# Four taps of chunk 6's depthwise convolution on TensorE, and the diagonals of chunk 7 made in another split

## The reference, cut to what matters

```python
def causal_depthwise_conv(x, buf, w, b):          # width 31, one filter per channel
    xp = jnp.concatenate([buf.astype(x.dtype), x], axis=1)
    y = lax.conv_general_dilated(xp, w[:, None, :], window_strides=(1,), padding='VALID',
                                 dimension_numbers=('NWC', 'WIO', 'NWC'), feature_group_count=ch)
    return y + b, xp[:, -(width - 1):, :]

def conformer_conv(h, buf, w_in, w_dw, b_dw, ln_g, ln_b, w_out):
    a, gate = jnp.split(h @ w_in, 2, axis=-1)
    u = a * jax.nn.sigmoid(gate)
    u, tail = causal_depthwise_conv(u, buf, w_dw, b_dw)
    u = layernorm(u, ln_g, ln_b)
    return jax.nn.silu(u) @ w_out, tail
```

## Time and profile before

| | us |
|---|---|
| median of 3 runs | 1502.82 |
| lowest, highest | 1500.53, 1505.07 |
| the profiled execution | 1500.38 |
| its span | 1498.8 |
| TensorE busy | 1458.5 (97%) |
| VectorE busy | 979.2 (65%) |
| ScalarE busy | 908.6 (61%) |

### The profile page before, as it was taken

The page is one execution under the profiler, slowest core; times in us unless marked ns, Lnnn a source line. Parts: engine busy times, 40 slices in busy tenths (PEclk is TensorE's granted clock), DMA queues, the critical chain, the costliest instruction groups (busy, mean ns, idle before and its releaser), DMA issues.

```text
span 1498.8 us, 28447 instructions
## 1 busy us (share of the span) xinstructions
PE 1458.5 (97%) x11276; PEld 1348.6 (90%) x11276; DVE 979.2 (65%) x1475; ACT 908.6 (61%) x1658; POOL 269.9 (18%) x469
## 2 busy tenths in 40 slices
PE   5999999999999999999999989999999999999998
PEld 4788669999999999999889856679999999999997
DVE  4799966878744878645546356664887744767643
ACT  4699877877633776535435556664767643666633
POOL 2489810000000332100000022210000000322200
PEclk9999999999999999999999999999999999999999
DMA  9887683355554454653437366653255554455653
GB/s 379 307 303 270 249 283 127 95 165 170 183 175 143 159 165 162 194 172 127 127 107 259 114 225 225 226 198 118 80 175 168 177 177 153 145 168 167 198 165 100
DMA packets 72118, 273.50 MB, mean 182 GB/s; under 512 B 8065, under 2 KB 10129, under 8 KB 71601
## 3 DMA queue, kind: packets, MB, share of 16 engines
q1 hardware_dynamic: 65824, 247.69, 49.0%
q0 software_dynamic: 5872, 23.64, 4.6%
q10 hardware_dynamic: 288, 0.35, 0.1%
HBM read 262.80 MB, written 8.85 MB: 181 GB/s over the span
## 4 chain that ended last, share of the span: by engine, by line
PE 85%; DVE 8%; ACT 3%; issue 2%; DMA 2%; SPq 0%; DVEq 0%; ACTq 0%
PE ps L739 68%; DVE ps L1896 4%; PE ps L1004 3%; PE ps L713 2%; PE ps L1076 1%; PE ps L1082 1%; PE ps L1059 1%; DMA ada_w<-w_ada_dram 1%; PE ps L1143 1%; PE ps L1095 1%; PE ps L1110 1%; PE ps L809 1%; PE ps L919 1%; ACT w_att L1631 1%; ACT w_hi L1287 1%
## 5 line engine op out<-in xcount | busy, mean ns | idle before, releaser
L1727 DVE TENSOR_TENSOR w_lo<-raw,w_hi 128x1024 fp32r<-128x1024 f32 (+1 forms) x296 | 387.4, 1310 | 229.5 <-ACT w_hi L1287 229.3
L739 PE MATMUL ps<-h_hi,w_hi 128*128 128x288 f32 x1920 | 524.9, 298 | 1.7 <-DVE h_lo L1801 1.7
L739 PE MATMUL ps<-h_lo,w_hi 128*128 128x288 f32 x1920 | 518.9, 294 | 0.0
L1287 ACT ACTIVATE w_hi<-raw 128x1024 fp32r<-128x1024 f32 (+1 forms) x309 | 347.0, 1124 | 108.1 <-PE ps L739 73.5
L739 PEld LDWEIGHTS ps<-h_hi,w_hi 128*128 128x128 f32 x1920 | 360.3, 188 | 7.9 <-DVE h_lo L1801 4.5
L739 PEld LDWEIGHTS ps<-h_lo,w_hi 128*128 128x128 f32 x1920 | 360.0, 187 | 1.1 <-issue 0.2
L739 PE MATMUL ps<-h_hi,w_lo 128*128 128x288 f32 x1920 | 312.4, 294 | 0.0
L739 PEld LDWEIGHTS ps<-h_hi,w_lo 128*128 128x128 f32 x1920 | 274.5, 188 | 0.0
L739 PE MATMUL ps<-act_hi,w_hi 128*128 128x288 f32 x704 | 193.2, 296 | 0.0
L739 PE MATMUL ps<-act_lo,w_hi 128*128 128x288 f32 x704 | 193.0, 297 | 0.0
L739 PEld LDWEIGHTS ps<-act_hi,w_hi 128*128 128x128 f32 x704 | 132.5, 188 | 0.0
(11 more groups left out here) (265 smaller groups left out, 2071.1 us busy)
## 6 DMA issues: line engine op xcount, KB each, us to landing
raw<-w_k_dram SPq DMA_DIRECT2D x245, 512.0 KB, 3.5
raw<-w_down_dram SPq DMA_DIRECT2D x64, 704.0 KB, 4.1
ada_w<-w_ada_dram SPq DMA_DIRECT2D x71, 512.0 KB, 5.8
k_page<-cache_kt_dram SPq DMA_DIRECT2D x32, 512.0 KB, 5.2
v_page<-cache_v_dram POOLq DMA_DIRECT2D x32, 512.0 KB, 5.1
ada_h<-w_ada_dram SPq DMA_DIRECT2D x7, 512.0 KB, 6.2
ada_u<-w_ada_dram SPq DMA_DIRECT2D x6, 512.0 KB, 15.1
ada_g<-w_ada_dram SPq DMA_DIRECT2D x6, 512.0 KB, 6.3
```

The lines of the kernel that those rows point to most:

```text
L739: return pe.matmul(ps[:, BANK[b], 0:HALF], lhsT=w[s][:, kb * P:(kb + 1) * P], rhs=v[:, at, :] if down else v[:, at, lo:hi], start=(at == 0 ...
L1287: act.activation(w_hi[SLOT[n]][:, 0:cols], raw[s][:, 0:cols], ACT.Copy).then_inc(s_hi, 1)
L1727: dve.tensor_tensor(w_lo[s][:, 0:cols], raw[n % RING][:, 0:cols], w_hi[s][:, 0:cols].bitcast(F32), ALU.subtract).then_inc(s_lo, 1)
```

## The change

The fifteen taps of chunk 7 stay on TensorE, and chunk 6 gets four there too, so VectorE has 18 taps of chunk 6 instead of 22. They are issued directly behind block 15, ahead of the four pieces. Both groups use bank 1, so the fifteen taps now also wait until VectorE has read the four taps' sum (its second tap of chunk 6), and the four wait until ScalarE has read the last gate from banks 0 and 1. VectorE's second tap of chunk 6 now needs TensorE's sum, so only one tap of chunk 6 remains ahead of `glu(7)`. Of the ten diagonals made during the blocks six are now chunk 7's and four chunk 6's; the other nine of chunk 7 are made behind block 15 (before: five).

```diff
-PE_TAPS = [0] * (C - 1) + [15]
+PE_TAPS = [0] * (C - 2) + [4, 15]
-DIAG_TILE = 10
-EARLY_TAPS = [13] + [9] * (C - 3) + [2, 0]
+DIAG_TILE = 6
+EARLY_TAPS = [13] + [9] * (C - 3) + [1, 0]
-        diag = place("diag", [P, DIAG_TILE, P], at=at)
+        diag = place("diag", [P, DIAG_TILE + PE_TAPS[C - 2], P], at=at)
             def conv_taps(i):
                 pe.wait_ge(pair_free[1], i + 1)
+                if i == C - 2:
+                    pe.wait_ge(pair_free[0], C)
+                else:
+                    pe.wait_ge(taps, TAP_DONE[C - 3] + TURNS_FROM[C - 2] + 1)
                 for k in range(PE_TAPS[i]):
-                    pe.wait_ge(diag_made, k + 1)
-                    d = diag[:, k, :] if k < DIAG_TILE else diag_more[:, k - DIAG_TILE, :]
+                    if i == C - 2:
+                        pe.wait_ge(diag_made, DIAG_TILE + k + 1)
+                        d = diag[:, DIAG_TILE + k, :]
+                    elif k < DIAG_TILE:
+                        pe.wait_ge(diag_made, k + 1)
+                        d = diag[:, k, :]
+                    else:
+                        pe.wait_ge(diag_made, PE_TAPS[C - 2] + k + 1)
+                        d = diag_more[:, k - DIAG_TILE, :]
+            conv_taps(C - 2)
             late_pieces(ADA_RING)
             conv_taps(C - 1)
             late_pieces(len(OWN_TILE))
                 if i in range(1, 6):
-                    for k in range(2 * i - 2, 2 * i):
-                        act.activation(diag[:, k, :], ident[:], ACT.Copy, scale=prm("w_a_dw", (C - 1) * WA + k))\
+                    for n in range(2 * i - 2, 2 * i):
+                        at, k = (C - 1, n) if n < DIAG_TILE else (C - 2, n - DIAG_TILE)
+                        act.activation(diag[:, n, :], ident[:], ACT.Copy, scale=prm("w_a_dw", at * WA + k))\
                             .then_inc(diag_made, 1)
```

## The result

The changed kernel takes 1504.48 us (median of 14 runs, 1501.84 to 1506.54), the kernel before 1501.53 us (14 runs, 1499.95 to 1505.07). The ratio is 1.0018 with a 95% interval of 1.0011 to 1.0025: slower by 1.7 to 3.8 us. The profiled execution took 1502.44 us (span 1500.8). The time lies in the predicted range and within 0.3% of before, but it moved up by 2.7 us where 0.2 us down was forecast.

What follows compares the result with a forecast made beforehand. TensorE, busy 1458.5 of 1498.8 us, bounds most; VectorE and ScalarE end this stage. Of 2.2 us off VectorE 0.2 arrives as TensorE becomes the bound: median 1502.6, range 1499.0 to 1505.5.

Steps and rivals of the forecast that it cites:

- They can start where the pieces started, at 163.90: TensorE behind block 15: four taps (3.49 us) start at 163.90, mostly filling 2.69 us idle; fifteen taps only 0.74 us later.
- the 195.40 that I forecast: Start of the square sums on TensorE, forecast at 195.40 instead of 195.62, 0.2 us earlier.
- The second rival: TensorE later still between block 15 and chunk 7's mean sum, hand-overs counting in full; up to +0.7 us, 1503.2; chance 0.20.
- its far end: Second rival's extreme: no cover, four taps only from 168.51, mean sum 4.6 us late, 1507.4; 0.03 of the 0.20.
- The mean sum of chunk 7 waits for nothing of VectorE's: Sign of being right: VectorE's last step ends near 190.7, at least 1.5 us before TensorE's mean sum of chunk 7.
- The new wait: Fifteen taps' wait for VectorE's bank 1 read: said to cost nothing, read ending 0.69 us before 169.25; a gap means wrong.
- VectorE idle at the reading tap: Sign of being wrong: VectorE waiting at its chunk 6 tap that reads TensorE's four-tap sum from bank 1.
- the 196.5 that I had set as the limit: Forecast as a whole is wrong if the square sums start before 194.4 or behind 196.5.
- with 0.26 us to spare: At the reading tap the four taps' sum is ready at 167.55 and VectorE comes at 167.81, so no wait.
- Nine diagonals: ScalarE behind block 15: nine diagonals in place of five add 1.17 us, ending its chunk 6 products at 179.99.
- The reduction at 180.47: VectorE's reduction of chunk 6's sample products, forecast to start at about 180.05, 2.2 us earlier, released by ScalarE.
- Nothing there: GpSimd and loads: ring loads issued up to 3.49 us later and `ada_g` loads still land in time, at no cost.

Runs made afterwards that it cites:

- before_again: The kernel before, unedited, run again for a second trace; median 1502.15 us, ratio 1.0001 to the kernel before.
- split_only: The kernel before with only the new split of the diagonals, chunk 6's four made during the blocks and used by nobody; 1501.64 us, ratio 1.0002.
- tensor_only: The kernel before with the diagonal split and chunk 6's four taps on TensorE, read by nobody; VectorE keeps its 22 taps; 1504.83 us, ratio 1.0019.
- small_before: The kernel before with the 48 adaLN loads used between the blocks cut to an eighth; 1501.18 us, ratio 0.9995.
- The two kernels with small loads: The kernel before and the changed kernel, each with the 48 adaLN loads between the blocks cut to an eighth; 1501.18 and 1501.13 us.
- pieces_first: The changed kernel with the four pieces directly behind block 15 and chunk 6's four taps behind them; 1506.06 us, ratio 1.0025 to the kernel before.
- after_again: The changed kernel, unedited, run again for a second trace; 1504.35 us, ratio 1.0016 to the kernel before.

## Why the prediction was wrong

**The point that failed: "They can start where the pieces started, at 163.90".** I took TensorE's place in one trace as a property of the kernel, and with it the 2.69 us of idle time that were to take up most of the 3.49 us. In the eleven traces with whole loads block 15 ends between 163.90 and 168.64, with 166.55 in the middle, and the trace that I read is the earliest of all. The first of the four-piece groups starts between about 45 and 48 us, and between it and block 15 TensorE's weight loads wait 2.4 to 6.5 us for DMAs.

**The sum with that put right.** The square sums start at the later of two things: TensorE's end, block 15 plus 31.34 us (three traces with whole loads: 31.34, 31.34, 31.35), and VectorE's, its last step plus 2.8 us (192.85 to 195.62, 193.29 to 196.08, 195.44 to 198.24). Without the four taps TensorE's is 31.34 - 3.49 = 27.85 us. VectorE's place is not fixed either. Its last wait for TensorE is at `glu(2)`, and from there its last step ends 112.25 us later where it has all its taps (112.24 to 112.25 in before, before_again, split_only, tensor_only and small_before). Its timeline in the first trace of the kernel before:

```profile
80.60 0.76 DVE L1927 TENSOR_TENSOR u_p<-ps,sig 128x288 f32<-128x288 f32 x2 [1.54 <-PE ps L713]
```

And in split_only, where block 15 ends latest:

```profile
83.19 0.76 DVE L1929 TENSOR_TENSOR u_p<-ps,sig 128x288 f32<-128x288 f32 x2 [3.25 <-PE ps L714]
```

(In the kernels with fewer taps on VectorE the last step comes sooner.) So lateness of TensorE ahead of `glu(2)` moves both engines, and only what it loses from there to block 15 uses up its slack. The two ends are equal when block 15 comes 112.25 + 2.78 - 31.34 = 83.69 us behind `glu(2)`; every us more is a us lost by the change. In the eleven traces it comes 83.30 to 86.07 us behind, and only the first trace of the kernel before lies below 83.69: there the sum gives 195.24, the 195.40 that I forecast but for 0.16 us, and a gain of 0.4 us. In the ten others it gives a loss of 0.4 to 2.4 us; the median of all eleven is 1.8 us lost, the mean 1.4. Of the 2.7 us measured (1.7 to 3.8) some 1.4 to 1.8 us are thus accounted for. For the rest I have no row. The two kernels with small loads are off in the same way: the sum gives the change 1.1 us of gain there, and the medians show 0.05. The intervals allow both, so the cause is shown and its size only in part.

**The second rival was the nearest, with the wrong reason, size and chance.** I gave it 0.20 and up to +0.7 us, for hand-overs between groups (1502.8 + 0.7 is 1503.5, not the 1503.2 written there, so the range should have ended at 1505.8). The hand-overs cost next to nothing: four taps took 168.36 - 164.84 = 3.52 us, not 3.49, the four pieces 1.86, and the whole stretch was 31.34, not the 31.50 that the forecast implies. What it lacked was its cause, TensorE arriving late, which its far end even priced (4.6 us, with no cover) and gave 0.03 "by the code". The code says only what TensorE waits for behind block 15, not when it gets there.

**TensorE's slack and the new wait.** The mean sum of chunk 7 waits for nothing of VectorE's, as said, and the fifteen taps wait for nothing (170.22 follows the pieces at once). The new wait binds only in pieces_first. VectorE idle at the reading tap, which I had named as a sign of being wrong, did appear (below). The square sums missed 195.4 by 0.8 us in the first trace, and in after_again, at 197.24, they lie beyond the 196.5 that I had set as the limit.

**VectorE.** I said it would not wait at the reading tap, with 0.26 us to spare. It waited 1.26 us, as the four taps began 0.94 us later and `glu(7)` came earlier than worked out (it ends at 167.28, not 167.81). Its last step gained 1.80 us, not 2.2. Neither mattered, since TensorE was later still.

**ScalarE.** Nine diagonals took 2.72 us in place of 1.56, +1.16 for 1.17 predicted, and split_only shows no cost for them. The reduction at 180.47 was not held by ScalarE, whose products of chunk 6 ended at 179.46; VectorE itself came later than 180.05. The table load began at 191.81, 1.78 us earlier (predicted 1.6).

**The loads.** "Nothing there" held for the `ada_g` loads. In the first trace of the changed kernel a piece near 209 us waits for its load, and the gap to the kernel before grows from 0.56 us at 205 to 1.2 us at 224. In after_again it does not. So that part is scatter, or at least not shown to be the change's. From the matmuls of L818 near 240 us to the end of the span the four traces of the two kernels take 1259.66 and 1261.38 us (before) and 1260.45 and 1260.61 us (changed), which scatters by more than the part that has no row. I also took 8.3 us, the longest landing of the six `ada_g` loads, for the longest of this size; the `ada_w` loads in the same trace go up to 17.3 us. The conclusion stands, as they had over 20 us.

**The cost of a tap.** The four taps took 3.52 us for eight instructions, 0.44 us each, as the thirty rows before had said. The Trainium skill's sustained 131 ns per matmul of 512 columns ("TensorE: Matmul & The Clock Gate", "Back-to-back issue gap") does not agree with these rows, and the measurement decides.

## What to carry to other kernels

A gap in front of an engine that is fed by loads is not free time of a known size: it is what absorbs the spread of that engine's arrival, and one trace shows one draw of it. Before filling a gap, take several traces, or ask how much later the engine could come before anything notices. Here that was 3.9 us in the first trace of the kernel before (195.62 - 163.90 - 27.85) and 1.4 us in the second, against 3.49 us of new work. Ask also what the other engine's place hangs on: lateness that moves both is harmless to the balance, lateness of one is not. And when an engine under one us behind the bound gets 3.5 us of new work, the question is not whether the old bound is relieved but what its own lateness is worth from then on.

## What the runs showed of the hardware

The same instructions of TensorE and the same loads put the end of block 15 anywhere in a window of 4.7 us in eleven traces (2.89 us apart in the two of the kernel before), while the whole kernel's time scatters by about 5 us and its median by well under 1. The loads of 512 KB into `ada_w` landed in 3.3 to 17.3 us in one and the same trace (median 5.8, the first of before), and the waits of TensorE's weight loads for such DMAs added up to 2.4 us in one execution and 6.5 us in another. The granted clock in the stretch was 1.00, the 2.4 GHz level, in the first traces of both kernels, so it has no part in the difference between these two. VectorE's 112 us from `glu(2)` to its last step, without a wait, repeat to 0.01 us in five traces.
